# The experts' second product as seven half-size products, summed token-major

## The reference, cut to what matters

```python
u = jnp.take(expert_u, eidx, axis=0)
act = jax.nn.gelu(jnp.einsum('thkd,td->thk', u, xb))
v = jnp.take(expert_v, eidx, axis=0)
return jnp.einsum('thk,thkd->td', gate * act, v)
```

## Time and profile before

| what | value |
|---|---|
| median of 3 runs | 3179.05 us (3177.11 to 3180.06) |
| the profiled execution's own time | 3180.33 us |
| its span (first to last instruction) | 3178.5 us |
| PE busy | 3062.0 us, 96% of the span |
| DVE busy | 2134.2 us, 67% |
| ACT busy | 1237.4 us, 39% |
| POOL busy | 861.5 us, 27% |
| granted TensorE clock, mean | 0.984 of full |

### The profile page before, as it was taken

The page is one execution under the profiler, slowest core; times in us unless marked ns, Lnnn a source line. Parts: engine busy times, 40 slices in busy tenths (PEclk is TensorE's granted clock), DMA queues, the critical chain, the costliest instruction groups (busy, mean ns, idle before and its releaser), DMA issues.

```text
span 3178.5 us, 38156 instructions
## 1 busy us (share of the span) xinstructions
PE 3062.0 (96%) x15318; PEld 2417.5 (76%) x15318; DVE 2134.2 (67%) x3453; ACT 1237.4 (39%) x1768; POOL 861.5 (27%) x550
## 2 busy tenths in 40 slices
PE   8889999999999999999999999999999999999997
PEld 4567777677777666878887788878888888888886
DVE  3678888768789766484989899466665444444445
ACT  3334444335333655324333466533223222233224
POOL 2233433222344210143455422322222110111100
PEclk9899999999999999999999999999999999999998
DMA  7221111334222111333244467766554333343341
GB/s 258 86 77 47 54 47 57 113 115 165 70 85 73 41 40 40 111 95 93 83 140 133 142 211 238 240 214 201 187 193 147 112 120 126 119 126 120 113 133 53
DMA packets 167568, 382.91 MB, mean 120 GB/s; under 512 B 10848, under 2 KB 77408, under 8 KB 167264
## 3 DMA queue, kind: packets, MB, share of 16 engines
q1 hardware_dynamic: 167392, 380.48, 37.3%
HBM read 320.14 MB, written 60.29 MB: 120 GB/s over the span
## 4 chain that ended last, share of the span: by engine, by line
PE 76%; DVE 15%; ACT 5%; POOL 2%; DMA 2%; issue 1%; SPq 0%; DVEq 0%; ACTq 0%; POOLq 0%
PE ps L738 21%; PE ps L740 20%; PE ps L739 20%; DVE oh L2409 2%; PE ps L1143 2%; DVE at L2147 2%; PE ps L1071 2%; DVE ai L2145 1%; PE ps L910 1%; PE ps L930 1%; PE ps L1051 1%; POOL wsp L2510 1%; PE ps L884 1%; POOL pk L2626 1%; DVE at L2135 1%
## 5 line engine op out<-in xcount | busy, mean ns | idle before, releaser
L738 PE MATMUL ps<-hT,wsp 128*128 128x512 f32 x2016 | 826.8, 410 | 39.5 <-POOL wsp L2510 27.4
L2510 POOL TENSOR_TENSOR wsp<-ring,wsp 128x1024 fp32r<-128x1024 f32 x207 | 513.9, 2486 | 1068.4 <-ACT wsp L1198 1032.6
L740 PE MATMUL ps<-hT,wsp 128*128 128x512 f32 x2016 | 792.5, 393 | 0.0
L739 PE MATMUL ps<-hT,wsp 128*128 128x512 f32 x2016 | 791.6, 393 | 0.0
L738 PEld LDWEIGHTS ps<-hT,wsp 128*128 128x128 f32 x2016 | 381.9, 189 | 146.3 <-issue 23.0
L740 PEld LDWEIGHTS ps<-hT,wsp 128*128 128x128 f32 x2016 | 381.8, 189 | 82.8
L739 PEld LDWEIGHTS ps<-hT,wsp 128*128 128x128 f32 x2016 | 382.8, 190 | 80.4 <-issue 8.6
L2633 POOL TENSOR_TENSOR ex<-ex 128x512 fp32r<-128x512 f32 x128 | 176.0, 1390 | 831.4 <-ACT ex L1593 831.4
L1198 ACT ACTIVATE wsp<-ring 128x1024 fp32r<-128x1024 f32 x311 | 321.9, 1051 | 97.1 <-PE ps L740 81.1
L2433 DVE TENSOR_TENSOR xT<-ps,xT 128x512 f32<-128x512 f32 x256 | 174.6, 687 | 260.5 <-PE ps L740 260.5
L738 PE MATMUL ps<-ex 128*128 128x512 f32 x808 | 314.8, 390 | 2.0 <-DVE ex L1653 2.0
(11 more groups left out here) (407 smaller groups left out, 4773.9 us busy)
## 6 DMA issues: line engine op xcount, KB each, us to landing
ring<-in_eu SPq DMA_DIRECT2D x128, 512.0 KB, 3.6
ring<-in_ev SPq DMA_DIRECT2D x128, 512.0 KB, 3.6
gd<-oh SPq DMA_DIRECT2D x8, 4096.0 KB, 14.9
ex<-gd SPq DMA_DIRECT2D x32, 1024.0 KB, 6.7
ring<-in_ein SPq DMA_DIRECT2D x57, 512.0 KB, 3.7
ring<-in_oin SPq DMA_DIRECT2D x39, 512.0 KB, 3.6
ex<-zd SPq DMA_DIRECT2D x17, 1024.0 KB, 9.1
ring<-in_ada SPq DMA_DIRECT2D x30, 512.0 KB, 3.6
```

What stands on the lines that cost most here:

```text
L738: pe.matmul(out, W[0], R[0], start=first, stop=False)
L739: pe.matmul(out, W[0], R[1], start=False, stop=False)
L740: return pe.matmul(out, W[1], R[0], start=False, stop=last)
L2510: pool.tensor_tensor(s[:, 1, :], raw_of(i), s[:, 0, :].bitcast(F32), ALU.subtract).then_inc(pool_done, G.step("lo", i))
```

## The change

Each chunk but the last takes another way through the second product. Its operands are cut in halves: AG (512 experts by 512 tokens) into four quarters of 256 by 256, V (512 experts by 1024 features) into four of 256 by 512. From them come seven products of a sum of quarters of AG with a sum of quarters of V, in place of the eight products of quarters that a plain block product needs. A product is 12 matmuls: two halves h of 128 tokens, two units j of 128 experts, three matmuls each. The result has tokens on the partitions and features along the columns.

Names in the new code, for chunk q, product i of 0 to 6, x = 7 q + i:

- `prep(x)` on DVE: the sums of quarters. `sadd` is a sum on the AG side (two at i = 0, one at i = 2, one at i = 3), `tadd` one on the V side (two each at i = 3, 4, 5, 6), all in place in raw tiles of 128 x 512.
- `prep(x)` on ACT: two roundings of the V side (`th`) and one of the AG side (`sh`), 128 x 512 each.
- `low(x)` on POOL: the two low parts of the V side. `left(x)` on DVE: the low part of the AG side.
- `vp(x)` on PE: the 12 matmuls. `vev(x)` on DVE: adds the two results to their sums in SBUF; three of the 14 results (`KEPT`) stay in PSUM through all chunks and are not evicted.
- `agp(q)`: the four gate multiplies of a chunk whose Z was stored. `zg(k)`: gelu and gate multiply of one unit made here. `zsplit`: rounding and low part of a unit of U; the low part is now POOL's for all units.

A product is prepared three ahead (`AHEAD`), in four operand buffers. The list for product x reads: `vev(x-1)`, perhaps a unit of z, `vp(x)`, `left(x+2)`, `prep(x+3)`, `low(x+3)`, and at i = 1 and 4 perhaps `zg` and `zsplit`. The chunks are reordered so that stored ones and computed ones alternate, and two units of z fall in each chunk. PSUM is cut into two banks for z, three for the products, three for the kept results.

The running sum `xT` is written to DRAM at the start of the expert stages, its SBUF serves for the sums, and it comes back in the end. The last chunk is done as before (`vs`), with its V split into `hT` (`vsplit`) and its AG into slots of U (`asplit`), both on ACT and POOL. While it runs, DVE combines the seven sums into four quarters (`comb`), PE turns them (`tc`, 32 transposes of 128 x 128), and DVE adds them to `xT` and to the last chunk's result (`vx`).

At the start of the stage the last gate store is cut in two: the part of the first two chunks is written at once, the rest later (`store_rest`). The six pre units there write to six tiles of their own and wait only for the stores of the 62 units before them.

```diff
-MORE = 5
+EXTRA = 4
+OPS = 4
+AHEAD = 3
+STORED_FIRST = 2
+PLEG = (3, 5, 0, 1, 2, 6, 4)
+ZA, ZB = 1, 4
+KEPT = ((3, 0), (3, 1), (2, 0))
...
-    for c in range(NC):
-        if c + 1 < NC:
-            order.extend(zs(c + 1))
-        if c + 2 < NC:
-            order.append(("gload", c + 2))
-        if c == NC - 1:
-            order += [("p_in",), ("freed", "np")]
-        order.append(("v", c, [unit("ev", c * JC + j) for j in range(JC)]))
...
+    seq = [0, 1, *(c for k in range(2, NPRE) for c in (k, NPRE - 2 + k))][:NC - 1] + [NC - 1]
+    end = NC - 1
...
+    def prep(x):
+        return [*([("left", x - 1)] if 0 < x <= 7 * end else []), *([("prep", x), ("low", x)] if x < 7 * end else [])]
...
+    order += [("ex_begin",), ("gload", 0), ("zload", 0), ("load_to", vn[0][1])]
+    for n, more in zip(last, between):
+        order += [("pre", z[0], n), *more]
+        z[0] += 1
     assert z[0] == NPRE * JC
-    first = len(units)
-    for c in range(NC):
-        if c + 1 < NC:
-            order.extend(zs(c + 1))
-        if c + 2 < NC:
-            order.append(("gload", c + 2))
-        if c == NC - 1:
-            order += [("p_in",), ("freed", "np")]
-        order.append(("v", c, [unit("ev", c * JC + j) for j in range(JC)]))
+    order += [z_step(0), ("load_to", zn[1])]
+    for x in range(7 * end):
+        q, i = divmod(x, 7)
+        k = 2 * q - 1 + (i == ZB)
+        here = i in (ZA, ZB) and 0 < k < len(zu)
+        if x:
+            order.append(("vev", x - 1))
+        if x in (7 * end - 7, 7 * end - 1):
+            order.append(("x_back", x == 7 * end - 1))
+        if x == 7 * end - 5:
+            order.append(("comb", 0))
+        if x == 7 * end - 1:
+            order.append(("comb", 1))
+        if here:
+            order.append(z_step(k))
+            if k == len(zu) - 1:
+                order.append(("freed", "np"))
+        order.append(("vp", x))
+        if x == ZB:
+            order.append(("agp", 1))
+        order += prep(x + AHEAD)
+        if i == ZA and 0 < q < end and seq[q + 1] < NPRE:
+            order.append(("agp", q + 1))
...
+            order += [("zg", 0)] * (k == 1) + [("zg", k)]
...
+        if q == end - 1:
+            order += {1: [("asplit", 0), ("asplit", 1)], 2: [("asplit", 2), ("vsplit", 0)], 3: [("asplit", 3), ("vsplit", 1)],
+                      4: [("vsplit", 2)], 5: [("vsplit", 3)]}.get(i, [])
+            if i == 3:
+                next_v(end, 3)
+                order.append(("load_to", vn[end][3]))
...
+        if i in (ZA, ZB) and 0 <= k < len(zu) - 1:
+            order.append(("zsplit", zn[k + 1]))
+            next_z()
...
+    order += [("load_to", pln[2]), ("vs", 0), ("vev", 7 * end - 1), ("comb", 2), ("comb", 3), ("vs", 1), ("vs", 2), ("tc", 0), ("tc", 1), ("vs", 3),
+              ("tc", 2), ("tc", 3), ("vx", 0, pln[0]), ("vs", 4), ("tc", 4), ("vx", 1, pln[0]), ("tc", 5), ("vx", 2, pln[0]),
+              ("tc", 6), ("tc", 7), ("vx", 3, pln[0]), ("p_in", 0)]
+    for m in range(4, 8):
+        order += [*([("vs", m + 1)] if m < 7 else []), ("vx", m, pln[0])]
+    order.append(("p_in", 1))
...
-                    or name == "eu" and u < NPRE * JC)
+                    or name == "eu")
...
+            lower, second = {0: (0, 0), 1: (1, 0), 2: (1, 1), 3: (0, 0), 4: (0, 1), 5: (1, 1), 6: (1, 0)}[i]
+            return raw_of(EV[q][2 * lower + j])[:, 512 * second:512 * second + 512]
...
+            late, second = {0: (0, 0), 1: (0, 1), 2: (0, 1), 3: (0, 0), 4: (1, 0), 6: (1, 1)}[i]
+            return agr[q % 3][:, 2 * second:2 * second + 2, 256 * late:256 * late + 256]
...
+            def vp(x):
+                q, i = divmod(x, 7)
+                W, R = left_op(x), right_op(x)
+                w.wait_ge(*right_low(x))
+                w.wait_ge(*left_low(x))
+                for h in range(2):
+                    kept = (i, h) in KEPT
+                    if not kept:
+                        out, free = v_b.open(("v", x, h), V, "ev", x, h)
+                        w.wait_ge(*free)
+                    elif q == 0:
+                        out, free = kept_b[KEPT.index((i, h))].open(("kept", i, h), V, "comb", 3)
+                        w.wait_ge(*free)
+                    else:
+                        out = sum_of[i, h]
+                    for j in range(2):
+                        m = slice(h * 128, h * 128 + 128)
+                        r = mm3(out, (W[:, 0, j, m], W[:, 1, j, m]), (R[:, 0, j, :], R[:, 1, j, :]),
+                                j == 0 and (q == 0 or not kept), j == 1 and (q == END - 1 or not kept))
+                    r.then_inc(tensor_done, T.step("vp", x, h))
...
+            def zg(k):
+                n = z_units[k][2]
+                w.wait_ge(tensor_done, T("use", n))
+                if k < 2:
+                    w.wait_ge(z_out[k % 2], 16 * NPRE * JC // 2)
+                else:
+                    w.wait_ge(vector_done, V("ag", *z_units[k - 2][0:2]))
+                act.activation(gl[k % 2], z_b.at[n], ACT.Gelu_apprx_tanh).then_inc(scalar_done, A.step("zgelu", n))
+            def prep(x):
+                q, i = divmod(x, 7)
+                if x >= OPS:
+                    w.wait_ge(tensor_done, T("vp", x - OPS, 1))
+                elif x == OPS - 1:
+                    w.wait_ge(st_out[1], 64)
+                for j in range(2):
+                    if i < 3:
+                        w.wait_ge(*landed(EV[q][2 * (i > 0) + j]))
+                    else:
+                        w.wait_ge(vector_done, V("tadd", x))
+                    act.activation(right_op(x)[:, 0, j, :], right_raw(x, j), ACT.Copy).then_inc(scalar_done, A.step("th", x))
+                if i in (0, 1, 6):
+                    w.wait_ge(vector_done, V("ag", q, JC - 1))
+                else:
+                    w.wait_ge(vector_done, V("sadd", x))
+                act.activation(left_op(x)[:, 0, :, :], left_raw(x), ACT.Copy).then_inc(scalar_done, A.step("sh", x))
...
+            def both(x, out, a, b, op):
+                for j in range(2):
+                    dve.tensor_tensor(out(j), a(j), b(j), op).then_inc(vector_done, V.step("tadd", x))
+            def prep(x):
+                q, i = divmod(x, 7)
+                x0 = 7 * q
+                right = lambda k: (lambda j: right_raw(x0 + k, j))
+                if i == 0:
+                    w.wait_ge(vector_done, V("ag", q, JC - 1))
+                    if q:
+                        w.wait_ge(*left_low(x - 2))
+                    dve.tensor_tensor(left_raw(x0 + 4), left_raw(x0), left_raw(x0 + 4), ALU.subtract).then_inc(
+                        vector_done, V.step("sadd", x0 + 4))
+                    w.wait_ge(vector_done, V("sadd", x0 + 4))
+                    dve.tensor_tensor(s2, left_raw(x0 + 6), left_raw(x0 + 4), ALU.subtract).then_inc(
+                        vector_done, V.step("sadd", x0 + 5))
+                if i == 2:
+                    w.wait_ge(*left_low(x0 + 1))
+                    w.wait_ge(vector_done, V("sadd", x0 + 5))
+                    dve.tensor_tensor(left_raw(x), left_raw(x0 + 1), s2, ALU.subtract).then_inc(vector_done, V.step("sadd", x))
+                if i == 3:
+                    w.wait_ge(*left_low(x0))
+                    dve.tensor_tensor(left_raw(x), s2, left_raw(x0), ALU.add).then_inc(vector_done, V.step("sadd", x))
+                    w.wait_ge(*right_low(x0))
+                    both(x, right(3), right(4), right(0), ALU.subtract)
+                if i == 4:
+                    w.wait_ge(vector_done, V("tadd", x0 + 3))
+                    w.wait_ge(*landed(EV[q][2]))
+                    w.wait_ge(*landed(EV[q][3]))
+                    both(x, right(4), right(2), right(4), ALU.subtract)
+                if i == 5:
+                    w.wait_ge(vector_done, V("tadd", x0 + 4))
+                    w.wait_ge(*right_low(x0 + 2))
+                    both(x, right(5), right(2), right(3), ALU.subtract)
+                if i == 6:
+                    w.wait_ge(vector_done, V("tadd", x0 + 5))
+                    w.wait_ge(*right_low(x0 + 1))
+                    both(x, right(6), right(5), right(1), ALU.subtract)
+            def left_low_part(x):
+                w.wait_ge(scalar_done, A("sh", x))
+                dve.tensor_tensor(left_op(x)[:, 1, :, :], left_raw(x), left_op(x)[:, 0, :, :].bitcast(F32), ALU.subtract).then_inc(
+                    vector_done, V.step("sl", x))
+            def vev(x):
+                q, i = divmod(x, 7)
+                for h in range(2):
+                    if (i, h) in KEPT:
+                        continue
+                    w.wait_ge(tensor_done, T("vp", x, h))
+                    acc = sum_of[i, h]
+                    if q == 0:
+                        w.wait_ge(xs_out, 16)
+                        dve.tensor_copy(acc, v_b.at["v", x, h]).then_inc(vector_done, V.step("ev", x, h))
+                    else:
+                        w.wait_ge(vector_done, V("ev", x - 7, h))
```

(61 more changed lines are left out.)

406 lines of the change are left out of this document (247 added, 159 removed).

## The result

The changed kernel takes 3385.2 us (median of 4, 3382.0 to 3387.9) against 3178.7 for the kernel before, now over 4 runs: ratio 1.0649 (95% interval 1.0633 to 1.0666). The forecast was 3382.

The account below looks back on a forecast made before the run. DVE and POOL excluding each other were taken to bound the changed kernel, PE following: 2071 + 36 + 29 x 39.3 + 38 + 27 = 3312 for the last add, +201, +2 after it, giving 3382 us; range 3205 to 3450.

Parts of the forecast that it names:

- two kinds of chunk: Loop chunks: 38.9 us for a chunk with z, 39.7 for the one in two also holding four stored gates.
- What bounds the kernel: Kernel before: PE busy 3062 of 3178.5 us, so a removed matmul is worth its time unless something else ends later.
- The exclusion: DVE instructions with both inputs in SBUF and POOL instructions do not run together; the later waits.
- The walk: Engine lists followed through one chunk with z, step by step: 38.9 us; mean with stored-gate chunks 39.3.
- The lock rule of the Trainium skill: DVE with two SBUF inputs and GpSimd block each other for the whole instruction; floor 38.7 us per chunk.
- the durations 33.8: Exclusive work per chunk from trace rows: POOL 22.4 plus DVE 11.4, together 33.8 us.
- Perfect turns: Rival: whenever DVE or POOL waits, the other has work; 33.8 us per chunk, total 3213; chance 0.22 including nearly perfect.
- steps 1, 3 and 4: Products of a chunk where DVE would wait for ACT with nothing else in its list; argued against perfect turns.
- The clock: Rival: PE's idle gaps lower its clock, costing 30 to 150 us, total above 3450; chance of that range 0.09.
- PE's busy share in the window: Sign that the forecast is right: PE busy share in the stage near 77%.
- PE's gap ahead of product 5: One long PE gap per chunk, some 6 us, waiting for a PSUM bank that DVE clears in step 5.
- The ends: Outside the loop: DVE enters step 0 at 2071, chunk 0 36 us, chunk 30 38, last chunk 27, then 2 more.

Follow-up runs that it names:

- e2: Changed kernel with POOL's 14 low parts per chunk on 32 of 512 columns, products reading the high part instead (result incomplete): 3106.9 us, ratio 0.9764 to the kernel before.
- after: The changed kernel itself, as profiled and measured, against the kernel before: 3385.2 us, ratio 1.0649.
- e1: Changed kernel with the 14 low parts of V's side per chunk moved from POOL to DVE: 3262.7 us, 35.1 us per chunk.
- e10: Against e7, POOL's five low parts per chunk no longer wait for DVE's sums of the next product; same instructions on the same engines: 3283.8 us.
- e3: Changed kernel with the first 12 matmuls of each of the 60 units of z made twice: 3386.7 us.
- e5: Changed kernel with POOL keeping five held-back V low parts per chunk, DVE making the others and U's, z units' gelu, gate, split one product later: 3350.4 us.
- e7: Against e5, ACT rounds the unit of U ahead of the roundings of product x+3, not behind them: 3185.3 us.
- e12: Against e7, two last-chunk splits on DVE, last-chunk splits listed later, product 0's sums ahead of product 6's low parts, POOL's product 6 wait changed: 3183.3 us.
- e11: Against e12, the four gate multiplies of a stored chunk spread over four products instead of in one piece: 3159.4 us, ratio 0.9933 to the kernel before.
- e9: Against e7, DVE makes all low parts of V's side and POOL none: 3223.2 us.

## Why the prediction was right

Its sum, term by term, with the trace of the changed kernel:

| term | predicted | measured |
|---|---|---|
| first product on PE | 2074 | 2074.0 |
| end of chunk 0 | 2107 | 2108.0 |
| chunks 1 to 29 | 29 x 39.3 = 1140 | 1131.4, 39.0 each |
| two kinds of chunk | 38.9 and 39.7 | 38.5 and 39.3 |
| chunk 30 | 38 | 40.7 |
| last chunk, to its last add | 27, at 3312 | 28.2, at 3308.3 |
| from there to the span's end, more than before | 2 | 71.9 - 68.1 = 3.8 |

- *What bounds the kernel.* Right: matmuls removed are worth their 0.2277 us each as long as nothing else ends later; e2 shows the gain, after shows what ended later.
- *The exclusion.* Right, and the decisive step: it came out of the maxima by line and the timelines where they fall. e1 takes POOL's turns away by moving them, e2 by shortening them, and e10 alone leaves all work in place and changes only their moment.
- *The closeness of the total* is in part luck. The 29 chunks came out 8 us shorter than predicted; chunk 0, chunk 30, the last chunk and what follows it 1.0, 2.7, 1.2 and 1.8 us longer, so most of it cancels.
- *The walk.* 39.3 against 39.0. The lock rule of the Trainium skill (SBUF — State Buffer, "SBUF: two separate sides") taken to the letter gave 38.7 as a floor, the durations 33.8. The near agreement of 38.7 with 39.0 is a coincidence: a turn inside POOL's stream shows 0.42 to 0.46 in the changed kernel as well (1.71 to 1.75 less 1.29). Added up from the trace over chunks 3 to 28, POOL or a DVE instruction with both inputs in SBUF is at work for 34.3 us of each 38.9, beside the predicted 33.8; in the other 4.7 neither is, and they wait for ACT or do adds from PSUM. e1's walk by the same rules gave 35.5, measured 35.1.
- *Perfect turns* (34 to 37 us per chunk, chance 0.22) did not come; its reason, DVE waiting for ACT in steps 1, 3 and 4, is there in the timeline, in the very steps named: in the chunk from 2602 to 2640 it is 0.60 and 2.28 us in step 1, 1.20 in step 3 and 1.80 in step 4, 5.9 in all, ahead of low parts and a gate.
- *The clock.* It fell to 0.91 in the stage, and e3 shows that this cost nothing. It also spoils one predicted sign: PE's busy share in the window is 65.5 of 78, 84%, not 77%, mostly since the ten or so matmuls behind a gap take longer: behind the one that ends at 2609.03 they start 0.43 us apart until 2613.5, which is the level of 1.2 GHz, and 0.23 from then on.
- *PE's gap ahead of product 5*, put down to the PSUM bank: the trace has it at 6.1 us, from 2602.9, released by DVE's eviction, but between the two halves of product 5, six of its matmuls later than predicted. It is a symptom, since e2 keeps the banks and loses the gap.

```profile
2609.03 0.80 PE L891 MATMUL ps<-ex 128*128 128x512 f32 x1 [6.10 <-DVE ex L2697]
```

- *The ends.* In chunk 30, short by 2.7 us, DVE combined the seven sums while POOL made the last splits, and two of these additions took 2.16 and 2.89 us in place of 0.68: the exclusion again, at a place where it had not been priced. Why the stretch behind the last add is 1.8 us longer than predicted, no run shows.

What was weaker came after. The expectations for e5 (missed by 170 us), e7 (by 25) and e12 (by 11) were sums of DVE's work with waits left out; the walk through the lists, which had served in the prediction, was not made with the same care. Open is what holds e7, e11 and e12 at 31.4 us in chunks without stored gates, 1.35 above TensorE's 30.05. Removing DVE's wait for ACT did not change it; in e12 the chain that ends last passes several times a chunk from TensorE to DVE's sums and ACT's roundings and back.

## What to carry to other kernels

Before work is put on POOL to relieve DVE, read the maxima of both by line, not the means, and look at the timeline where they fall. Here 1.77 and 1.76 us came within 0.25 of the sum of two instructions' own times, 0.69 and 1.29: the engines share something. A DVE instruction that meets POOL then costs 1.1 us more (1.75 against 0.61), and POOL's help can cost more than it takes over: the 14 low parts made on POOL took 3.9 us a chunk more than on DVE itself (39.0 against 35.1). In this kernel such work paid where it ran mostly beside DVE's adds from PSUM, and it needed a wait that put it there; without the wait it cost.

A reduction of a product's matmuls by 12.5% that adds some 17 instructions on DVE and 12 on POOL per chunk has to be priced on those first. And a new order can bring waits of its own: the largest single step here (165 us) was the repair of one that e5 had brought in, one rounding's place in ACT's list.

## What the runs showed of the hardware that had not been expected

- The moment of POOL's turns decides whether they help or harm. Against none at all (e9, 3223.2), the same five low parts per chunk save 38 us when a wait holds them back (e7) and cost 60 us when it is left out (e10). A wait that orders two engines is worth 98.5 us, 3% of this kernel.
- From the third chunk on the changed kernel's period is steady to 0.1 us (38.5 and 39.3 to 39.4 in turn, but for one of 39.6), although the two engines contend all the time, while in e10 it wanders from 33.5 to 37.5.
- TensorE did 720 matmuls more in the same time at a higher granted clock, 0.98 against 0.91 in the window: filling its gaps was free. The expectation had named this as possible and not relied on it.
